# Two transformer-like blocks in one kernel: reordering around its weight chunks and modulation pairs

## What is computed

```python
mod = jax.nn.silu(c) @ ada_w + ada_b                  # 1024 -> 6144, for each of the three blocks
sh_m, sc_m, gt_m, sh_f, sc_f, gt_f = split(mod, 6)
h = rms_norm(x, g_pre_mix) * (1.0 + sc_m) + sh_m
proj = h @ w_in
...
x = x + gt_m * rms_norm(merged @ w_out, g_post_mix)
h = rms_norm(x, g_pre_mlp) * (1.0 + sc_f) + sh_f
f = jnp.square(jax.nn.relu(h @ w1)) @ w2
x = x + gt_f * rms_norm(f, g_post_mlp)
```

## Time and profile before

| | |
|---|---|
| median of three executions | 1735.22 us (1732.3 to 1739.69) |
| profiled execution | 1738.21 us, its span 1736.4 us |
| granted TensorE clock, mean | 0.985 |
| PE matmul busy | 1648.1 us (95%) |
| PE weight load busy | 1570.4 us (90%) |
| DVE busy | 1108.8 us (64%) |
| ACT busy | 813.8 us (47%) |
| POOL busy | 34.0 us (2%) |
| DMA | 331.40 MB, 191 GB/s in the mean |

### The profile page before, as it was taken

One profiled execution on the slowest core, in us unless ns is written; L12 is line 12 of the kernel. 1 busy time (PEld: TensorE's weight loads), 2 busy tenths in 40 slices (PEclk: granted clock), 3 DMA queues, 4 the chain that ended last, 5 costly groups with the idle time before them and its releaser, 6 DMA issues.

```text
span 1736.4 us, 34270 instructions
## 1 busy us (share of the span) xinstructions
PE 1648.1 (95%) x15182; PEld 1570.4 (90%) x15182; DVE 1108.8 (64%) x1400; ACT 813.8 (47%) x1057; POOL 34.0 (2%) x68
## 2 busy tenths in 40 slices
PE   5998999999998999999998999999999999989997
PEld 4996888799996999999997999979999999979996
DVE  3577744788946464678867545565546877665464
ACT  3346324433334536458544435444544675445352
POOL 0001000000000000000001000000000000000000
PEclk8999999999998999999999999999999999999998
DMA  9437444744546546445558655554454545735552
GB/s 390 159 123 264 151 178 180 269 166 165 203 175 229 170 147 194 157 170 182 173 193 346 235 189 194 188 208 171 151 189 146 195 170 175 267 117 193 193 189 81
DMA packets 45529, 331.40 MB, mean 191 GB/s; under 512 B 5072, under 2 KB 5072, under 8 KB 5456
## 3 DMA queue, kind: packets, MB, share of 16 engines
q1 hardware_dynamic: 36032, 260.73, 43.6%
q0 software_dynamic: 9216, 67.11, 9.9%
q10 hardware_dynamic: 144, 1.51, 0.2%
HBM read 326.18 MB, written 1.05 MB: 188 GB/s over the span
## 4 chain that ended last, share of the span: by engine, by line
PE 74%; DVE 12%; ACT 8%; DMA 4%; issue 2%; SPq 1%; POOL 0%; ACTq 0%; DVEq 0%; POOLq 0%
PE ps L397 19%; PE ps L399 19%; PE ps L398 19%; DVE w_lo L1652 5%; PE ps L450 4%; ACT w_hi L1109 4%; DMA raw<-stream 2%; PE ps L525 2%; DMA ada_alt<-ada 1%; PE ps L693 1%; PE ps L682 1%; DVE rsq L2420 1%; DMA ada_raw<-ada 1%; DVE rstd L1699 1%; PE ps L501 1%
## 5 line engine op out<-in xcount | busy, mean ns | idle before, releaser
L397 PE MATMUL ps<-act_hi,w_hi 128*128 128x256 f32 x2672 | 756.7, 283 | 17.6 <-DVE act_lo L1728 4.6
L1652 DVE TENSOR_TENSOR w_lo<-raw,w_hi 128x2048 fp32r<-128x2048 f32 x207 | 474.4, 2292 | 448.9 <-ACT w_hi L1109 448.3
L398 PE MATMUL ps<-act_lo,w_hi 128*128 128x256 f32 x2672 | 747.6, 280 | 0.0
L399 PE MATMUL ps<-act_hi,w_lo 128*128 128x256 f32 x2672 | 747.4, 280 | 0.0
L1109 ACT ACTIVATE w_hi<-raw 128x2048 fp32r<-128x2048 f32 (+1 forms) x229 | 421.8, 1842 | 513.4 <-PE ps L399 496.1
L397 PEld LDWEIGHTS ps<-act_hi,w_hi 128*128 128x128 f32 x2672 | 506.2, 189 | 24.7 <-issue 13.6
L398 PEld LDWEIGHTS ps<-act_lo,w_hi 128*128 128x128 f32 x2672 | 507.6, 190 | 0.7
L399 PEld LDWEIGHTS ps<-act_hi,w_lo 128*128 128x128 f32 x2672 | 506.3, 189 | 0.0
L397 PE MATMUL ps<-mlp_hi,w_hi 128*128 128x256 f32 x512 | 141.8, 277 | 0.4
L398 PE MATMUL ps<-mlp_lo,w_hi 128*128 128x256 f32 x512 | 141.4, 276 | 0.0
L399 PE MATMUL ps<-mlp_hi,w_lo 128*128 128x256 f32 x512 | 141.4, 276 | 0.0
(11 more groups left out here) (442 smaller groups left out, 1991.9 us busy)
## 6 DMA issues: line engine op xcount, KB each, us to landing
raw<-stream SPq DMA_DIRECT2D x233, 1024.0 KB, 4.9
ada_raw<-ada POOLq DMA_DIRECT2D x46, 1024.0 KB, 6.6
ada_alt<-ada POOLq DMA_DIRECT2D x12, 1024.0 KB, 12.0
ada_f<-ada POOLq DMA_DIRECT2D x6, 1024.0 KB, 8.8
ada_f<-ada SPq DMA_DIRECT2D x4, 1024.0 KB, 15.0
ada_a<-ada SPq DMA_DIRECT2D x3, 1024.0 KB, 20.8
s<-s SPq DMA_DIRECT2D x4, 512.0 KB, 10.1
consts_stage<-consts_a SPq DMA_DIRECT2D x1, 1728.0 KB, 33.1
```

The lines of the kernel that those rows point to most:

```text
L397: mm(out, ah, bh, start=first, stop=False, skip_group_check=shared)
L398: mm(out, ah, bl, start=False, stop=False, skip_group_check=shared)
L399: return mm(out, al, bh, start=False, stop=last, skip_group_check=shared)
L1652: tt(w_lo[:, s2, :], raw[:, s4, :], w_hi[:, s2, :].bitcast(f32), ALU.subtract).then_inc(S("lo_ready"), 1)
```

## The change

The arithmetic stays the same; pieces of work are done in another order, and eight matmuls on constants are added. Part by part:

1. **Chunk 0 in halves.** SP loads chunk 0 as two DMAs, each with half of the columns of both output blocks (the first four k-steps, then the last four). ACT makes `w_hi` of it in two copies, ahead of the modulation, and `w_hi` of chunk 1 after it. DVE makes the first half of `w_lo` before it waits for the first modulation, the second half between steps of the modulation. The third quarter of the small transposes (L569) stands before the last of the eight tiles. Two matmuls of 512 columns on constants (`keep_warm`) precede chunk 0. The vectors for the context (`mod_ctx`) are computed after `w_lo` of chunk 2.
2. **Keys and values.** DVE runs `conv_kv(c-1)` before, not after, the `w_lo` of chunk c+4, and ACT prepares chunk 9 before `th_kv`.
3. **Constants of the layers.** ACT issues the load of `consts_b` (1472 KB) at the start of the output projection, not at the start of layer 0.
4. **Down.** ACT prepares chunk 38 before the last tanh and the last two `mid_hi` copies of the up stage. Pair 18 is computed between chunks 37 and 38, and `ada_tr(2)` comes eight blocks into chunk 38, not two. `ada_rows(2)` and `ada_out(2)` of ACT follow one chunk later.
5. **Pairs.** The batches, buffers and load order of pairs 18 to 31 are new. After the down stage come pairs 19, 20 and 21, 22; in layer 0 before the MLP 23, 24 and 25 with `keep_warm(2, 5)`; then 26, 27 as before, and 28 with `keep_warm(2, 0)`; in layer 1 before the MLP 29, `ada_tr(6)`, `keep_warm(2, 5)`, then 30 and 31. `ada_tr` of the MLP's batches goes from after the second chunk of the MLP to its 27th. In layer 1 the last four columns of the scale are added (`mods_scale`) just before the modulation of the MLP.

```diff
-        ADA_BATCH = ((0, 8, 0), (8, 5, 0), (13, 5, 6), (18, 4, 6), (22, 4, 6), (26, 4, 6), (30, 2, 6))
-        ADA_SECOND = (15, 17, 19, 21, 23, 25, 27, 29, 31)
+        ADA_BATCH = ((0, 8, 0), (8, 5, 0), (13, 6, 6), (19, 4, 6), (23, 3, 6), (26, 3, 6), (29, 1, 6), (30, 2, 6))
+        ADA_SECOND = (15, 17, 20, 22, 24, 27, 30)
...
-            load(0, 0)
+            for hf, sem in ((0, "part_moved"), (1, "raw_loaded0")):
+                sp.dma_start(k_half(raw[:, 0, :], hf), k_half(io["stream"][stream_index(0)], hf)).then_inc(S(sem), 16)
...
+            def keep_warm(n, bank):
+
+                for _ in range(n):
+                    mm(ps[:, bank, :], ident, cc[:, :], start=True, stop=True)
...
-            begin(N_Q, 0)
-            mod_chunk(N_Q % 2, 0, 1, 0).then_inc(S("chunk_done"), 1)
+            keep_warm(2, 6)
+            mod_chunk(N_Q % 2, 0, 1, 0, N_Q + 1).then_inc(S("chunk_done"), 1)
...
-                if at_ == 34:
+                if at_ == 32:
+                    ada_mm(18)
+                if at_ == 40:
                     ada_tr(2)
...
                 norm_folded(2 + 2 * L, ns + 1, a6)
-                ada_mm(22 if L == 0 else 30)
+                ada_mm(23 if L == 0 else 29)
                 if L == 0:
-                    ada_mm(23)
+                    ada_mm(24)
+                else:
+                    ada_tr(6)
+                    keep_warm(2, 5)
                 norm(ns + 2, a6)
-                ada_mm(24 if L == 0 else 31)
+                ada_mm(25 if L == 0 else 30)
                 if L == 0:
-                    ada_mm(25)
+                    keep_warm(2, 5)
+                else:
+                    ada_mm(31)
...
             act.wait_ge(S("conv"), 1)
             act_(th_kv[:, :, :, :], y_kv[:, :, :, :], ACT.Tanh, scale=0.5)
-            prep(N_UZ + 3, (N_UZ + 3) % RAW, (N_UZ + 3) % 2)
...
             prep(N_OUT1 + 1, (N_OUT1 + 1) % RAW, (N_OUT1 + 1) % 2)
+            act.dma_start(cu[:, 0:N_CB], io["consts_b"]).then_inc(S("consts_loaded"), 16)
...
+            prep(N_DOWN + 2, (N_DOWN + 2) % RAW, N_DOWN % 2)
             up_tanh(FB // 4 * 4, FB % 4)
...
             for c in range(4):
+                if c > 0:
+                    conv_kv(c - 1)
                 job(N_KV + c, 1)
                 if c == 0:
                     conv_q()
-                else:
-                    conv_kv(c - 1)
```

More of the change, by code:

```diff
@@ L433, in out_chunk, with mod_chunk @@
                 return last
-            def mod_chunk(wp, bank, s, m):
+            def mod_chunk(wp, bank, s, m, rest=None):
                 for k in range(KT):
                     pe.wait_ge(S("mod_lo"), 8 * m + k + 1)
+                    if k == 4 and rest is not None:
+                        pe.wait_ge(S("lo_ready"), rest)
                     for b in range(2):
@@ L565, in _ @@
                     last.then_inc(S("mod_rows_mm"), 1)
-                for q in {3: (0,), 5: (1,), 7: (2, 3)}.get(m, ()):
+                for q in {3: (0,), 5: (1,), 6: (2,), 7: (3,)}.get(m, ()):
                     pe.wait_ge(S("mod_rows_ev"), q + 1)
@@ L1084, in _ @@
                         deep_chunk((n + 8 + c) % 2, c, hf, ready=all_ready if c == 0 else None).then_inc(S("chunk_done"), 1)
+                        if hf == 1 and c == 2:
+                            ada_tr(4 + 3 * L)
                 norm_folded(3 + 2 * L, ns + 3, a6)
@@ L1209, in _ @@
                 act_(mod_rows[:, q * 512:(q + 1) * 512], ps[:, 1 + q, :], ACT.Copy).then_inc(S("mod_rows_ev"), 1)
-            prep(0, 0, 0)
+            for hf, sem, n_done, done in ((0, "part_moved", 16, "half_hi"), (1, "raw_loaded0", 16, "hi_ready")):
+                act.wait_ge(S(sem), n_done)
+                act_(k_half(w_hi[:, 0, :], hf), k_half(raw[:, 0, :], hf), ACT.Copy).then_inc(S(done), 1)
+            mod_hi(0, norm_h1, None, act_hi[1])
             prep(1, 1, 1)
-            mod_hi(0, norm_h1, None, act_hi[1])
             for c in range(2):
@@ L1633, in _ @@
                             prep(m + 1, (m + 1) % RAW, (m + 1) % 2)
+                        if hf == 1 and c == 3:
+                            ada_out(4 + 3 * L)
                         if hf == 1 and c % 2 == 1:
@@ L1707, in square_sum, with pipe @@
                     tt(sq[:, 0, :], sq[:, 0, :], sq[:, 1, :], ALU.add).then_inc(S("norm_pre"), 1)
-            def pipe(m, pre, lo):
+            def pipe(m, pre, lo, between=None):
                 for b in range(KT + 2):
+                    if b == 4 and between is not None:
+                        between()
                     if b < KT:
@@ L1779, in _, with first_lo, second_half @@
             marks.append(rs(1, xc, xc))
+            def first_lo(hf):
+                return tt(k_half(w_lo[:, 0, :], hf), k_half(raw[:, 0, :], hf), k_half(w_hi[:, 0, :], hf).bitcast(f32), ALU.subtract)
+            def second_half():
+                dve.wait_ge(S("hi_ready"), 1)
+                first_lo(1).then_inc(S("lo_ready"), 1)
+            dve.wait_ge(S("half_hi"), 1)
+            first_lo(0)
             dve.wait_ge(S("mod_mm"), 1)
             both = ps[:, 5, 0:32].rearrange("p (c a) -> p a c", a=2)
-            order(tt(mod_ctx[:, :], both[:, 1, :], V("b_ada", 16), ALU.add))
             tt(mod[:, 0:16], both[:, 0, :], V("b_ada", 16), ALU.add).then_inc(S("mods_done"), 1)
             dve.wait_ge(S("mods_done"), 1)
-            order(stt(gs[:, 0, :], mod_ctx[:, 8:16], 1.0, V("g_pre_mix", KT), ALU.add, ALU.mult))
             order(stt(gs[:, 1, :], mod[:, 8:16], 1.0, V("g_pre_mix", KT), ALU.add, ALU.mult))
-            prep(0, 0, 0)
             dve.wait_ge(S("dve_order"), marks[1][1])
-            scale_shift(0, norm_h1, gs[:, 1, :], mod[:, 0:8], act_hi[1], act_lo[1])
+            scale_shift(0, norm_h1, gs[:, 1, :], mod[:, 0:8], act_hi[1], act_lo[1], second_half)
             prep(1, 1, 1)
@@ L1794, in _ @@
             job(N_Q, 1)
+            order(tt(mod_ctx[:, :], both[:, 1, :], V("b_ada", 16), ALU.add))
+            order(stt(gs[:, 0, :], mod_ctx[:, 8:16], 1.0, V("g_pre_mix", KT), ALU.add, ALU.mult))
             scale_shift(1, xc, gs[:, 0, :], mod_ctx[:, 0:8], act_hi[0], act_lo[0])
```

80 lines of the change are left out of this document (45 added, 35 removed).

## The result

Twelve executions of the changed kernel took 1729.99 us in the median (1723.92 to 1735.24), twelve of the kernel before 1740.28 us (1732.3 to 1747.15). The ratio is 0.9938, 95% interval 0.9916 to 0.9960: 10.8 us faster (7 to 15), where the sum had 17.2. The profiled execution took 1735.24 us, the slowest of the twelve. It is only 3.0 faster than the profiled one of before (1738.21), so the stages have to be compared one by one.

The account below looks back on a forecast made before the run. PE bounds the kernel (74% of the chain), so gains were sought in its waits and half-clock stretches. Terms summed to −17.2 from 1738.21: 1721.0, or 1718.2 as median; forecast 1719.5 us, range 1711 to 1728.

Parts of the forecast that it names:

- start: Chunk 0 in halves: gain waited out before chunk 2, later context vectors cost 0.4; +0.4 us (−0.5 to +2.1).
- keys and values: Idle 2.27 and half clock at chunk 8 go, then `y_kv` limits the first transposes; −3.0 us (−1 to −3.3).
- chunk 14: Output projection: constants loaded there may delay raw tile 14; +0.5 us (0 to +3.7).
- down: Down stage: chunk 38 starts 0.45 earlier, the half-clock stretch doesn't come (−3.4); −3.9 us (−0.5 to −3.9).
- entry of layer 0: Pair 22's last tile lands about 3.5 earlier without the constants, so the next chunk starts earlier; −5.5 us (0 to −7).
- MLP of layer 0: Modulated chunk ends 2.2 earlier, `ada_tr` no longer waits 0.78; −2.9 us (−1 to −2.9).
- entry of layer 1: Pair 29 becomes `keep_warm`, next chunk bound by DVE's `w_lo` either way; 0 us (−0.3 to +0.5).
- MLP of layer 1: As in layer 0: modulated chunk ends 2.2 earlier, `ada_tr` about 0.6; −2.8 us (−1 to −2.8).
- half-clock bound (+2.1): Upper bound at the start: new idle before chunks 1 and 2 brings a half-clock stretch of +1.7 us.
- rule of turns between the queues: Chunk 14: DMA engines serve queues in turn, so constants slow tile 14 only by their share; 0 instead of 0.5 us.
- half clock comes back elsewhere: Rival: shortened idle times still bring four half-clock stretches of 1.7; −9.5 instead of −17.2, 1727 us; chance 0.13.
- slow rival: New idle at chunks 1 and 2 keeps 1.2 GHz through keys and values; 1744 us or more; chance 0.03.

Follow-up runs that it names:

- e12: The changed kernel run once more as it is; ratio 0.9923 (0.9894 to 0.9953) to the kernel before, median 1727.5 us.
- e7: The changed kernel without its eight constant matmuls (`keep_warm`); ratio 0.9932 (0.9907 to 0.9958) to the kernel before.
- e8: The kernel before with only `w_hi` of chunk 38 made ahead of the last tanh and `mid_hi`; ratio 0.9971 (0.9952 to 0.9990) to the kernel before.
- e3: The changed kernel with part 3 undone, `consts_b` loaded by ACT at the start of layer 0; ratio 0.9964 (0.9946 to 0.9982) to the kernel before.

## Why the prediction was wrong

The kernel got faster, in the main for the reasons given, but 1729.99 lies above the range's 1728, and the gain is 10.8 where 17.2 was the sum. Two steps failed, of about the same size: the base (5.1) and the sum (6.4).

**The base.** I set the forecast against the median of three runs, 1735.22, "3.0 below the profiled one". Twelve runs have 1740.28, and the groups beside the experiments 1738.35 to 1743.45: the profiled execution was on the fast side of them, not the slow one. 0.9938 of 1735.22 would be 1724.5, inside the range. With a spread of 15 us among executions three of them fix a base to no better than some 3 us (an estimate from the twelve), and my range left out that width.

**The sum**, stage by stage, profile of after against that of before (the stage from the first transposes to chunk 10, +7.4 and not in the forecast, is left out):

| step | forecast | measured | |
|---|---|---|---|
| start | +0.4 | +0.4 | from chunk 2 on; up to +2.3 with half clock |
| keys and values | −3.0 | −2.0 | up to the first transposes |
| chunk 14 | +0.5 | 0.0 | |
| down | −3.9 | −2.4 | up to the start of chunk 46 |
| entry of layer 0 | −5.5 | −3.7 | chunk 46 to chunk 49; −6.2 where no half clock fell on it |
| MLP of layer 0 | −2.9 | −2.0 | −0.9 in e12 |
| entry of layer 1 | 0 | −0.1 | −1.0 for the pair, +0.9 for the pace |
| MLP of layer 1 | −2.8 | −1.6 | −1.8 in e12 |
| sum | −17.2 | −11.4 | |

- *Start:* right in both parts, the covered gain and the 0.4. The half-clock bound (+2.1) was about right, and the stretch came in four of twelve profiles. But `keep_warm` was priced at 1.1, at most 2.3: it took 1.98 at full clock and 3.76 here, at half clock. The rows count each of these f32 matmuls twice, and I had taken the four records of 1.13 for four matmuls. It cost nothing only because the landing of chunk 2 covered it here and DVE's steps in the layers (e7).
- *Keys and values:* "the end of `y_kv` is what is late next" was wrong. `y_kv` ended at 127.04 and PE started on it at 127.68, behind chunk 9. That chunk had waited 0.99 for `uz`, an eviction queued on ACT behind the two tanh, which I had moved in the sum without asking who waits behind them. Without that wait `y_kv` would have been next, only 0.6 earlier. The slow pace took 0.4 more.
- *Chunk 14:* the bytes were through at 302.50, before tile 14 was issued at 302.66. So the rule of turns between the queues was not put to the test, and the 0 came from the lead of almost 7 us.
- *Down:* chunk 38's start (−0.84 against −0.45) and the half clock avoided (−3.0 against −3.4) were right. What failed was "3.4 less" as a stage's gain: the chunks behind took 5.65 and not 5.44, +1.5 up to chunk 46. They did so in all profiles with the change and no ticks there, and in e8. In the one profile of before they had been at the fast pace; whether that kernel usually has it there isn't known.
- *Entry of layer 0:* the constants had been issued 1.2 us ahead of the tiles, so only what was left of them stood before the last tile: 2.56, and 3.2 in e3, not 3.5 plus. And the half clock at this place, which the forecast let go with the idle time, came in seven of fourteen profiles with the constants moved, in four of them for 6.8 us (39.2 to 39.8 for the entry, against 35).
- *MLPs:* "ends 0.7 after the last `act_lo`" used the price of the last step alone. The last three `act_lo` come 0.4 apart and PE takes 0.68 for each, so the chunk ends 1.4 behind the last. That is 1.2 gained in layer 0 and 0.8 to 1.0 in layer 1, instead of 2.2 twice. The 0.8 for `ada_tr` was right, but its new place brings the slow pace for the five chunks behind it, about 0.9 in layer 0. In layer 1 part of the MLP was slow before the change as well, and the stretch got no longer.

The rival *half clock comes back elsewhere* was partly what happened, at the entry of layer 0. One reading in it was wrong: the clock did not fall after the 1.62 of idle. That idle time ends at 557.60 and follows two others of 1.02 and 1.41; the clock fell at 556.57, in the middle of it. And the 0.86 for faster by more than 0.5% doesn't come out of the terms named for it, which give 0.82. The slow rival, half clock in the first chunks, showed its beginning (6.8 us in e12) and never grew.

## What to carry to other kernels

Price an idle time by what stands right behind it as well: the work that queued behind the moved instruction on its own engine (`uz` behind the tanh), the pace at which several late operands are taken up (three steps 0.4 apart, 0.68 each), and the pace at which the dense stretch behind it will run. Compare profiles stage by stage, and over several executions, before you believe a difference between two totals: here 7.4 us of the wrong sign stood in a stage that nobody had touched, half-clock stretches for the most part. Set a forecast against a base with its spread, not against three runs.
